# The causal mask of two softmax attentions: a bf16 product on TensorE, or an addition on VectorE

## The chip, the cores and the metric

The kernel runs on one core of a Trainium2 chip. The metric is the device time of one execution in microseconds; the time before is the median of three runs, 904.34 us.

## What is computed

The reference is two hybrid layers in a row on 512 tokens of width 1024. The first mixes a forgetting attention of 8 heads, a pooling branch and a stick-breaking attention of 4 heads; the second mixes an MLA attention of 8 heads with a gated convolution, and then has a feed-forward net. The change touches the two softmax attentions only. Their scores are masked before the softmax:

```python
def forgetting_attention(q, k, v, log_f):
    c = jnp.cumsum(log_f, axis=-1)
    def one_block(args):                      # 128 queries
        qi, ci, i = args
        qpos = i * Q_BLOCK + jnp.arange(Q_BLOCK)
        sc = jnp.einsum('bhqd,bhkd->bhqk', qi, k).astype(jnp.float32) * scale
        sc = sc + (ci[..., :, None] - c[..., None, :])
        sc = jnp.where(kpos[None, :] <= qpos[:, None], sc, NEG)
        p = jax.nn.softmax(sc, axis=-1)
        return jnp.einsum('bhqk,bhkd->bhqd', p.astype(v.dtype), v)

def causal_block_attention(q, k, v):          # the MLA attention, 128 queries a block
    s = jnp.einsum('bqhd,bkhd->bhqk', q_blk, k).astype(jnp.float32) * scale
    s = jnp.where(k_idx[None, :] <= q_idx[:, None], s, jnp.finfo(jnp.float32).min)
    pr = jax.nn.softmax(s, axis=-1)
    return jnp.einsum('bhqk,bkhd->bqhd', pr.astype(v.dtype), v)
```

## The kernel before

Every engine has its own program, written out by hand, and semaphores tie them together. Large products are three fp32r products of split operands (L502, L503, L504: high by high, low by high, high by low). The weights stream from HBM through SyncE's queue; GpSimd splits them into high and low parts (L447, L455) ahead of TensorE.

Each softmax attention is `softmax_attention`, once in the program of TensorE, once in that of ScalarE, once in that of VectorE. It goes over 32 steps `m` (8 heads by 4 blocks of 128 queries); step n counts both attentions together, 0 to 31 for the forgetting attention ("fox") and 32 to 63 for MLA. A step has `kw` = 128, 256, 384 or 512 keys in turn, since a block of queries sees the keys up to its own. The last 128 of them are the diagonal block, the only one that the mask cuts.

In a step TensorE does `scores(m)` (for fox three products L806, L807, L808; for MLA L1079; and then the mask, L726), `turn_probs(m - 3)` (as many 128x128 transposes, L559, as the block has key blocks), and `beside(m)`: three products of another matrix (L502 to L504) that fill the time. After every two heads comes `values` (L747). For the first three steps of an attention there is nothing to transpose. The scores lie in banks 0 to 2 in turn, the transposed probabilities in banks 3 and 4.

VectorE takes the negated maximum of the scores (L2003), and after it, for the step before, the reciprocal of the sum (L2009) and the product with it (L2010, `h`). Besides these it does what is hung between the steps (`fox_pair`, `mix_low`, `sqk_out`, `mla_pair`). ScalarE takes the exponential out of the bank with its sum (L1462, two records) and then copies the transposed probabilities of the step three back out of their bank (L1324, `PT<-bank` or `arena<-bank`). The waits that matter: the maximum waits for `scored` of its step, the exponential for `maxed`, the reciprocal for `exped`, the transposes of a step for `normed` of that step and for `pt_made` of the step two back, the scores for `exped` of the step three back.

The mask is made once by GpSimd (L411, L420): 0 where a key may be seen, -1e30 above the diagonal, in bf16. `ident_b` is the identity in bf16, so the product L726 adds the mask to the bank.

Of the kernel before, what the change touches and what calls it, by code (L numbers as in the profile page):

```python
# [7 lines left out]
P = 128  # L8
F32 = mybir.dt.float32
F32R = mybir.dt.float32r  # L10
BF16 = mybir.dt.bfloat16
# [11 lines left out]
HD = 64  # L23
# [170 lines left out]
def hybrid_kernel(nc, x_d, w_d, cols_d, pos_d, wpool_d, pt_d, gains_d, out_d):  # L194
    tiles = tile_counts(psum_tiles())
    with ExitStack() as ctx:
# [33 lines left out]
        c_head = sb("c_head", [P, FOX_H], F32R)  # L230
        ident = sb("ident", [P, P])
        ident_b = sb("ident_b", [P, P], BF16)
        mask_le = sb("mask_le", [P, P], BF16)
        mask_lt = sb("mask_lt", [P, P], BF16)
        neg_tri = sb("neg_tri", [P, P])
        neg_one = sb("neg_one", [P, P])
# [94 lines left out]
        sines = sem("sines")  # L331
        angles = sem("angles")

        scored, maxed, exped, normed = sem("scored"), sem("maxed"), sem("exped"), sem("normed")
        turned, pt_made, pv_done, pv_drained = sem("turned"), sem("pt_made"), sem("pv_done"), sem("pv_drained")

        z_full, z_abs, z_exp, z_ln, sp_made = sem("z_full"), sem("z_abs"), sem("z_exp"), sem("z_ln"), sem("sp_made")
# [148 lines left out]
        def _(pe):  # L486
# [226 lines left out]
            def softmax_attention(base, heads, score_, v_, beside, first=None, tail=None):  # L713
                steps = heads * T

                def scores(m):
                    i, qb = m // T, m % T
                    n = base + m
                    if m >= 3:
                        pe.wait_ge(exped, n - 2)  # L720
                    elif first:
                        first(m)
                    out = bank[n % 3]
                    kw = (qb + 1) * P
                    score_(out[:, 0:kw], i, qb, kw)
                    mm(out[:, qb * P:kw], ident_b[:, :], mask_le[:, :], start=False, stop=True).then_inc(scored, 1)  # L726

                def turn_probs(m):
                    qb = m % T
# [72 lines left out]
            def fox_score(out, i, qb, kw):  # L802

                at = slice(qb * P, (qb + 1) * P)
                c_at = 0 if qb < 2 else S // 2
                mm(out, q_parts[:, i, at], k_parts[:, i, 0:kw], start=True, stop=False)  # L806
                mm(out, q_swapped[:, i, at], k_parts[:, i, 0:kw], start=False, stop=False)  # L807
                mm(out, c_head[0:HD + FOX_H, i:i + 1].broadcast_to([HD + FOX_H, P]),  # L808
                   c_parts[0:HD + FOX_H, c_at:c_at + kw], start=False, stop=False)

            pe.wait_ge(k_lo, FOX_H)
            pe.wait_ge(q_swapped_in, 32)
# [263 lines left out]
                    out2a_block(0, g, k)  # L1076

            def mla_score(out, i, qb, kw):
                mm(out, q2T[0:QK2, i, qb * P:(qb + 1) * P], k2T[0:QK2, i, 0:kw], start=True, stop=False)  # L1079

            softmax_attention(FOX_H * T, MLA_H, mla_score, v2, out2c_piece,
                              first=lambda m: pe.wait_ge(drained["act"], tiles["q2T", 2][3][1]),
# [711 lines left out]
        def _(dve):  # L1794
# [201 lines left out]
            def softmax_attention(base, heads, pair_out, beside=None, ahead_of_last=None):  # L1996
                steps_ = heads * T
                for m in range(steps_ + 1):
                    if m < steps_:
                        n = base + m  # L2000
                        kw = (m % T + 1) * P
                        dve.wait_ge(scored, n + 1)
                        V.tensor_reduce(negmax[:, n % 8:n % 8 + 1], bank[n % 3][:, 0:kw], AX_X, ALU.max, negate=True)\  # L2003
                            .then_inc(maxed, 1)
                    if m > 0:
                        n = base + m - 1
                        kw = ((m - 1) % T + 1) * P
                        dve.wait_ge(exped, n + 1)
                        own(V.reciprocal(erec[:, n % 8:n % 8 + 1], esum[:, n % 8:n % 8 + 1]))  # L2009
                        V.tensor_scalar(P_buf[:, n % 4, 0:kw], P_buf[:, n % 4, 0:kw], erec[:, n % 8:n % 8 + 1],  # L2010
                                        None, ALU.mult).then_inc(normed, 1)

                    if m % (2 * T) == T + 1 and m > 2 * T:
                        pair_out(m // (2 * T) - 1)
                    if beside is not None:
                        beside(m)
                if ahead_of_last is not None:
                    ahead_of_last()
                pair_out(heads // 2 - 1)
# [463 lines left out]
```

## Time and profile before

| | us |
|---|---|
| median of 3 runs | 904.34 (904.05 to 904.45) |
| the profiled execution, its own time | 904.17 |
| its span, first to last instruction | 902.4 |
| TensorE busy in it | 895.1 (99%) |
| VectorE, ScalarE, GpSimd busy | 390.9, 342.4, 496.0 |
| granted clock of TensorE | 1.00 |
| fox attention, first to last mask | 147.5 to 201.7 |
| MLA attention, first to last mask | 391.3 to 447.2 |

The first number of a row of the timeline is the start in us from the span's start, the second the record's length. A record of TensorE is longer than what it keeps the engine: products overlap, and what a product costs is read from the start of one to the start of the next.

### The profile page before, as it was taken

To read this page: it belongs to the slowest core of one execution; us is meant where nothing else is said; L and a number is where in the kernel's file an instruction comes from. 1 tells how busy PE (TensorE), PEld (TensorE's weight loads), DVE (VectorE), ACT (ScalarE), POOL (GpSimd) and SP (SyncE) were. 2 spreads that over 40 slices of the span, in tenths; PEclk is the share of its full clock that TensorE was granted. 3 is DMA by queue.
4 is the path that set the end of the run, shared out by engine and by line. 5 is a ranking of instruction groups with operands and counts; after the bars stand their busy time and mean duration, and the time that the engine had idled before them with its cause. 6 is when DMAs were issued, how large, how long until landed. Compare 5 with 4: busy or idle time off the path is not lost. (4 is left out here: it accounts for less than half of the span.)

```text
span 902.4 us, 12927 instructions
## 1 busy us (share of the span) xinstructions
PE 895.1 (99%) x4528; PEld 737.3 (82%) x4528; DVE 390.9 (43%) x684; ACT 342.4 (38%) x693; POOL 496.0 (55%) x515
## 2 busy tenths in 40 slices
PE   8999999999999999999999999999999999999998
PEld 7889887777779888876679988888888888888887
DVE  2753494667743652755657611111111122223672
ACT  4333403556726221565648522222222223223421
POOL 7987794311565877923236454444444455555453
PEclk9999999999999999999999999999999999999999
DMA  6335522103122322321012332222232322222213
GB/s 218 120 137 130 141 104 94 47 25 117 72 70 71 117 98 90 110 77 47 12 48 97 107 136 93 93 93 93 100 105 97 117 94 93 93 96 105 74 53 117
DMA packets 28412, 85.73 MB, mean 95 GB/s; under 512 B 5064, under 2 KB 8016, under 8 KB 28240
## 3 DMA queue, kind: packets, MB, share of 16 engines
q1 hardware_dynamic: 24528, 78.65, 25.3%
q10 hardware_dynamic: 3840, 6.48, 2.5%
q8 instruction: 29, 0.48, 0.2%
q14 instruction: 15, 0.12, 0.1%
HBM read 80.93 MB, written 2.10 MB: 92 GB/s over the span
## 5 line engine op out<-in xcount | busy, mean ns | idle before, releaser
L455 POOL TENSOR_TENSOR w_lo<-raw,w_hi 128x256 fp32r<-128x256 f32 (+1 forms) x420 | 409.2, 1002 | 206.5 <-ACT w_hi L1324 200.6
L502 PE MATMUL bank<-aT_hi,w_hi 128*128 128x512 f32 (+1 forms) x584 | 225.7, 387 | 0.0
L504 PE MATMUL bank<-aT_hi,w_lo 128*128 128x512 f32 (+1 forms) x584 | 222.4, 381 | 0.0
L503 PE MATMUL bank<-aT_lo,w_hi 128*128 128x512 f32 (+1 forms) x584 | 222.2, 381 | 0.0
L502 PE MATMUL bank<-w_hi,aT_hi 128*128 128x512 f32 (+3 forms) x576 | 218.5, 379 | 0.7 <-POOL w_lo L455 0.7
L504 PE MATMUL bank<-w_hi,aT_lo 128*128 128x512 f32 (+3 forms) x576 | 213.2, 370 | 0.0
L503 PE MATMUL bank<-w_lo,aT_hi 128*128 128x512 f32 (+3 forms) x576 | 212.9, 370 | 0.0
L447 POOL TENSOR_SCALAR w_hi<-raw 128x1024 fp32r<-128x1024 f32 x70 | 76.3, 1091 | 180.2 <-PE bank L504 143.9
L1324 ACT ACTIVATE w_hi<-raw 128x1024 fp32r<-128x1024 f32 x70 | 74.2, 1060 | 232.2 <-PE bank L504 220.0
L504 PEld LDWEIGHTS bank<-aT_hi,w_lo 128*128 128x128 f32 x584 | 109.8, 188 | 21.0
L503 PEld LDWEIGHTS bank<-aT_lo,w_hi 128*128 128x128 f32 x584 | 110.0, 188 | 19.9 <-issue 0.2
L502 PEld LDWEIGHTS bank<-aT_hi,w_hi 128*128 128x128 f32 x584 | 110.0, 188 | 19.7 <-issue 0.2
L502 PEld LDWEIGHTS bank<-w_hi,aT_hi 128*128 128x128 f32 x576 | 108.5, 188 | 19.3 <-issue 1.6
L504 PEld LDWEIGHTS bank<-w_hi,aT_lo 128*128 128x128 f32 x576 | 108.3, 188 | 18.4
L503 PEld LDWEIGHTS bank<-w_lo,aT_hi 128*128 128x128 f32 x576 | 108.6, 189 | 16.0
L2339 DVE TENSOR_TENSOR aT_lo<-arena,aT_hi 128x512 fp32r<-128x512 f32 x22 | 27.3, 1250 | 78.0 <-ACT aT_hi L1324 78.0
L2328 DVE TENSOR_TENSOR arena<-arena,bank 128x512 f32 (+1 forms) x22 | 15.1, 688 | 93.4 <-PE bank L504 90.6
L2325 DVE TENSOR_TENSOR arena<-bank,R 128x512 f32<-128x512 f32 x22 | 15.2, 692 | 88.3 <-PE bank L504 87.8
L1462 ACT ACTIVATE h<-bank,negmax 128x128 f32<-128x128 f32 (+1 forms) x64 | 33.9, 529 | 44.4 <-DVE negmax L2003 43.9
L2003 DVE TENSOR_REDUCE negmax<-bank 128x1 f32<-128x128 f32 (+1 forms) x64 | 31.1, 488 | 34.9 <-PE bank L726 33.8
L1324 ACT ACTIVATE arena<-bank,stat 128x512 f32<-128x512 f32 (+3 forms) x32 | 19.6, 612 | 45.4 <-PE bank L504 42.3
L1810 DVE SCALAR_TENSOR_TENSOR aT_lo<-bank,g_col,aT_hi 128x256 fp32r<-128x256 f32 (+3 forms) x41 | 20.4, 527 | 23.8 <-ACT aT_hi L1324 22.0
(235 smaller groups left out, 921.6 us busy)
## 6 DMA issues: line engine op xcount, KB each, us to landing
raw<-in_weights SPq DMA_DIRECT2D x141, 512.0 KB, 3.2
q_swapped<-q_parts ACTq DMA_DIRECT2D x2, 1024.0 KB, 12.5
x<-in_x ACTq DMA_DIRECT2D x4, 512.0 KB, 5.2
y_out<-x SPq DMA_DIRECT2D x7, 256.0 KB, 4.0
x<-in_x SPq DMA_DIRECT2D x3, 512.0 KB, 7.8
g_post<-in_gains ACTq DMA_DIRECT2D x3, 512.0 KB, 3.4
x<-in_x SPq DMA_DIRECT2D x2, 256.0 KB, 3.7
raw<-in_weights SPq DMA_DIRECT2D x2, 256.0 KB, 4.7
```

What stands on the lines that cost most here:

```text
L447: nc.gpsimd.tensor_scalar(w_hi[:, s, :], raw[:, r, :], 1.0, 1.0, ALU.mult, ALU.mult).then_inc(hi_made, 1)
L455: lo = nc.gpsimd.tensor_tensor(w_lo[:, s, at], raw[:, r, at], w_hi[:, s, at].bitcast(F32), ALU.subtract)
L502: mm(out, st_hi, mv_hi, start=start, stop=False)
L503: mm(out, st_hi, mv_lo, start=False, stop=False)
L504: return mm(out, st_lo, mv_hi, start=False, stop=stop)
L1324: return A(out, in_, ACT.Copy, scale=scale)
L1462: A(P_buf[:, n % 4, 0:kw], bank[n % 3][:, 0:kw], ACT.Exp, bias=negmax[:, n % 8:n % 8 + 1], accum_out=esum[:, n % 8:n % 8 + 1]).then_inc(ex ...
L1810: return V.scalar_tensor_tensor(out=out, in0=in0, scalar=scalar, in1=in1, op0=op0, op1=op1)
L2003: V.tensor_reduce(negmax[:, n % 8:n % 8 + 1], bank[n % 3][:, 0:kw], AX_X, ALU.max, negate=True)\
L2325: V.tensor_tensor(sg_t[:, slot, :], bank[2 * slot][:, :], R[:, :], ALU.mult).then_inc(ffn_scaled, 1)
L2328: V.tensor_tensor(act[:, bass.ds(f, 1), :], sg_t[:, slot, :].unsqueeze(1), bank[2 * slot + 1][:, :].unsqueeze(1), ALU.mult).then_inc(ffn_a ...
L2339: V.tensor_tensor(aT_lo[:, slot, :].unsqueeze(1), act[:, bass.ds(k, 1), :], aT_hi[:, slot, :].bitcast(F32).unsqueeze(1), ALU.subtract).the ...
```

## The change

The product L726 goes, and with it the last weight load of each score. The last product of the scores itself closes the group and signals `scored`: `fox_score` and `mla_score` now return it. `mask_le` becomes fp32. In VectorE's program each step now begins with an addition of the mask, in place, onto the last 128 columns of the bank, and the maximum waits for it by a new semaphore, `masked`. The same product of the stick-breaking attention (`mask_lt`, L829) stays.

```diff
-        mask_le = sb("mask_le", [P, P], BF16)
+        mask_le = sb("mask_le", [P, P])
...
-                    score_(out[:, 0:kw], i, qb, kw)
-                    mm(out[:, qb * P:kw], ident_b[:, :], mask_le[:, :], start=False, stop=True).then_inc(scored, 1)
+                    score_(out[:, 0:kw], i, qb, kw).then_inc(scored, 1)
...
-                mm(out, c_head[0:HD + FOX_H, i:i + 1].broadcast_to([HD + FOX_H, P]),
-                   c_parts[0:HD + FOX_H, c_at:c_at + kw], start=False, stop=False)
+                return mm(out, c_head[0:HD + FOX_H, i:i + 1].broadcast_to([HD + FOX_H, P]),
+                          c_parts[0:HD + FOX_H, c_at:c_at + kw], start=False, stop=True)
...
-                mm(out, q2T[0:QK2, i, qb * P:(qb + 1) * P], k2T[0:QK2, i, 0:kw], start=True, stop=False)
+                return mm(out, q2T[0:QK2, i, qb * P:(qb + 1) * P], k2T[0:QK2, i, 0:kw], start=True, stop=True)
...
                         dve.wait_ge(scored, n + 1)
+                        own_keys = bank[n % 3][:, kw - P:kw]
+                        V.tensor_tensor(own_keys, own_keys, mask_le[:, :], ALU.add).then_inc(masked, 1)
+                        dve.wait_ge(masked, n + 1)
                         V.tensor_reduce(negmax[:, n % 8:n % 8 + 1], bank[n % 3][:, 0:kw], AX_X, ALU.max, negate=True)\
                             .then_inc(maxed, 1)
```

In the changed kernel line numbers are higher by one from L334 on and by three behind the addition: L2003 becomes L2006, and the addition is L2004.

TensorE, fox steps 3 and 4, before:

```order
L808 MATMUL bank0<-c_parts,c_head 128x512
L726 MATMUL bank0<-mask_le,ident_b 128x128
L559 MATMUL bank3<-ident,h 128x128
L502 MATMUL bank7<-aT_hi,w_hi 128x512
L503 MATMUL bank7<-aT_lo,w_hi 128x512
L504 MATMUL bank7<-aT_hi,w_lo 128x512
L806 MATMUL bank1<-k_parts_51,q_parts_50 128x128
L807 MATMUL bank1<-k_parts_51,q_swapped_52 128x128
L808 MATMUL bank1<-c_parts,c_head 128x128
L726 MATMUL bank1<-mask_le,ident_b 128x128
L559 MATMUL bank4<-ident,h 128x128 x2
```

and in the changed kernel:

```order
L808 MATMUL bank0<-c_parts,c_head 128x512
L560 MATMUL bank3<-ident,h 128x128
L503 MATMUL bank7<-aT_hi,w_hi 128x512
L504 MATMUL bank7<-aT_lo,w_hi 128x512
L505 MATMUL bank7<-aT_hi,w_lo 128x512
L806 MATMUL bank1<-k_parts_51,q_parts_50 128x128
L807 MATMUL bank1<-k_parts_51,q_swapped_52 128x128
L808 MATMUL bank1<-c_parts,c_head 128x128
L560 MATMUL bank4<-ident,h 128x128 x2
```

The transposes now stand right behind the last product of the scores; nothing else moved.

VectorE, the end of fox (steps 28 to 31), before:

```order
L2003 TENSOR_REDUCE negmax<-bank2 128x1
L2009 RECIPROCAL erec<-esum 128x1
L2010 TENSOR_SCALAR h<-h,erec 128x128
L2026 TENSOR_TENSOR arena<-bank6,arena 128x512
L1842 TENSOR_TENSOR aT_lo<-arena,aT_hi 128x512
L2003 TENSOR_REDUCE negmax<-bank0 128x1
L2009 RECIPROCAL erec<-esum 128x1
L2010 TENSOR_SCALAR h<-h,erec 128x256
L2003 TENSOR_REDUCE negmax<-bank1 128x1
```

and in the changed kernel:

```order
L2004 TENSOR_TENSOR bank2<-bank2,mask_le 128x128
L2006 TENSOR_REDUCE negmax<-bank2 128x1
L2012 RECIPROCAL erec<-esum 128x1
L2013 TENSOR_SCALAR h<-h,erec 128x128
L2029 TENSOR_TENSOR arena<-bank6,arena 128x512
L1842 TENSOR_TENSOR aT_lo<-arena,aT_hi 128x512
L2004 TENSOR_TENSOR bank0<-bank0,mask_le 128x128
L2006 TENSOR_REDUCE negmax<-bank0 128x1
L2012 RECIPROCAL erec<-esum 128x1
L2013 TENSOR_SCALAR h<-h,erec 128x256
L2004 TENSOR_TENSOR bank1<-bank1,mask_le 128x128
L2006 TENSOR_REDUCE negmax<-bank1 128x1
```

Each maximum has an addition in front of it; the order is otherwise the same.

## Rows read from the trace of the kernel before

**Rows 1.** The page, busy time, share of the span and instructions of each engine.

```profile
PE 895.1 (99%) x4528; PEld 737.3 (82%) x4528; DVE 390.9 (43%) x684; ACT 342.4 (38%) x693; POOL 496.0 (55%) x515
```

**Rows 2.** Timeline of TensorE in fox: start, length, line, out<-in; mask products of two steps.

```profile
152.64 0.27 PE L807 MATMUL bank<-k_parts,q_swapped 128*128 128x128 f32 x1
152.75 0.27 PE L808 MATMUL bank<-c_parts,c_head 72*128 72x128 f32 x1
...
157.80 0.23 PE L726 MATMUL bank<-mask_le,ident_b 128*128 128x128 bf16 x1
157.87 0.28 PE L559 MATMUL bank<-ident,h 128*128 128x128 f32 x1
...
158.22 0.40 PE L503 MATMUL bank<-aT_lo,w_hi 128*128 128x512 f32 x1
```

**Rows 3.** Timeline of TensorE, transposes without a mask product ahead.

```profile
16.07 1.04 PE L559 MATMUL bank<-ident,x 128*128 128x128 f32 x8
...
17.17 0.39 PE L503 MATMUL bank<-w_lo,aT_hi 128*128 128x512 f32 x1
```

**Rows 4.** Timeline of TensorE in MLA, a step with one transpose.

```profile
401.94 0.22 PE L726 MATMUL bank<-mask_le,ident_b 128*128 128x128 bf16 x1
...
402.34 0.39 PE L503 MATMUL bank<-w_lo,aT_hi 128*128 128x512 f32 x1
```

**Rows 5.** Timeline of TensorE, bf16 mask products back to back.

```profile
208.80 0.62 PE L829 MATMUL bank<-mask_lt,ident_b 128*128 128x128 bf16 x8
```

**Rows 6.** Groups of VectorE by form: count, busy us, mean ns, idle us before them.

```profile
L2339 DVE TENSOR_TENSOR aT_lo<-arena,aT_hi 128x512 fp32r<-128x512 f32 x22 | 27.3, 1250 | 78.0 <-ACT aT_hi L1324 78.0
L2328 DVE TENSOR_TENSOR arena<-arena,bank 128x512 f32 x18 | 12.4, 688 | 85.8 <-PE bank L504 85.8
...
L2003 DVE TENSOR_REDUCE negmax<-bank 128x1 f32<-128x128 f32 x16 | 4.6, 289 | 14.7 <-PE bank L726 13.9 <-ACT arena L1443 0.8
...
L2064 DVE TENSOR_TENSOR sp_sum<-PT 128x128 f32<-128x128 f32 x2 | 0.6, 291 | 0.1
```

**Rows 7.** Timeline of VectorE, an instruction that waits for the one before it.

```profile
158.68 0.15 DVE L2009 RECIPROCAL erec<-esum 128x1 f32<-128x1 f32 x1
158.87 0.42 DVE L2010 TENSOR_SCALAR h<-h,erec 128x384 f32<-128x384 f32 x1
```

**Rows 8.** Waits in fox, 147 to 205 us: total us, times, longest.

```profile
DVE negmax L2003 <- PE bank L726: 15.1, 18, 2.5
```

**Rows 9.** Waits in MLA, 391 to 449 us.

```profile
DVE negmax L2003 <- PE bank L726: 18.6, 21, 2.4
```

**Rows 10.** Timeline of ScalarE at the start of fox.

```profile
148.89 1.28 ACT L1479 ACT_TABLE_LOAD   x1
...
153.89 0.27 ACT L1324 ACTIVATE PT<-bank 128x128 f32<-128x128 f32 x1
```

**Rows 11.** Timeline of VectorE at the start of fox.

```profile
150.87 0.78 DVE L2010 TENSOR_SCALAR h<-h,erec 128x128 f32<-128x128 f32 x1
...
152.49 0.68 DVE L2003 TENSOR_REDUCE negmax<-bank 128x1 f32<-128x512 f32 x1
```

**Rows 12.** Timeline of TensorE, the transposes of step 2.

```profile
154.30 0.52 PE L559 MATMUL bank<-ident,h 128*128 128x128 f32 x3
```

**Rows 13.** Timeline of VectorE at the end of fox, maximum of step 30.

```profile
200.41 0.55 DVE L2003 TENSOR_REDUCE negmax<-bank 128x1 f32<-128x384 f32 x1
```

**Rows 14.** Timeline of ScalarE at the end of fox, copy of step 27.

```profile
201.57 0.59 ACT L1324 ACTIVATE PT<-bank 128x512 f32<-128x512 f32 x1
```

**Rows 15.** Timeline of TensorE at the end of fox, transposes of step 29.

```profile
202.59 0.38 PE L559 MATMUL bank<-ident,h 128*128 128x128 f32 x2
```

**Rows 16.** Timeline of VectorE at the start and at the end of MLA.

```profile
392.59 0.16 DVE L1833 TENSOR_TENSOR stat<-stat 128x4 f32<-128x4 f32 x1 [4.59 <-ACT stat L1331]
...
446.64 0.56 DVE L2003 TENSOR_REDUCE negmax<-bank 128x1 f32<-128x384 f32 x1 [0.17 <-DVE arena L2226]
```

**Rows 17.** Timeline of TensorE at the end of MLA, transposes of step 61.

```profile
448.54 0.41 PE L559 MATMUL bank<-ident,h 128*128 128x128 f32 x2 [0.27 <-ACT PT L1324]
```

More of the change, by code:

```diff
@@ L332, in hybrid_kernel @@
         angles = sem("angles")
-        scored, maxed, exped, normed = sem("scored"), sem("maxed"), sem("exped"), sem("normed")
+        scored, masked, maxed = sem("scored"), sem("masked"), sem("maxed")
+        exped, normed = sem("exped"), sem("normed")
         turned, pt_made, pv_done, pv_drained = sem("turned"), sem("pt_made"), sem("pv_done"), sem("pv_drained")
```

## The prediction

> **What bounds the kernel now.** The page comes first: TensorE is busy 99% of the span [rows 1], so the time is TensorE's work plus its few gaps, and every other engine matters only where TensorE comes to wait for it. The timeline of TensorE then shows both attentions without a gap but one, of 0.27 us at the end of MLA [rows 17]. So a step costs what TensorE issues in it. The waits show the other side: the maxima of VectorE wait for the scores for 15.1 us in the 32 steps of fox [rows 8] and for 18.6 us in those of MLA [rows 9], 0.47 and 0.58 us a step. That is the room for what VectorE is given, if it is where it is needed.
>
> **What goes from TensorE.** 64 products of 128 columns with their weight loads. From the start of a mask product to the start of the second product behind it are 0.42 us in fox with one transpose between [rows 2]. Without a mask product ahead, eight transposes and one such product take 1.10 us [rows 3]. With 0.23 us for a 512-column product that is (1.10 - 0.23) / 8 = 0.11 us a transpose and nothing over. So the mask costs 0.42 - 0.11 - 0.23 = 0.08 us, on finer reading 0.074 in every such step of fox; in MLA 0.40 - 0.34 = 0.06, finer 0.064 [rows 4]. [...] At 128 keys in fox less comes free: L807 and L808 start 0.11 us apart [rows 2], twice what 128 columns take [rows 5], so the weight load sets the pace, and the load of the next transpose would show where the mask hid it. I count 0.025 us there. MLA: 32 x 0.064 = 2.05 us, and 0.15 more for its first three steps, where no transposes stand between. Fox, steps 4 to 31: 21 x 0.074 + 7 x 0.025 = 1.7 us. Steps 0 to 3 would give 0.4 us but give nothing: the first exponential waits for a table load that ends at 150.17, and through the reciprocal the product of step 0 ends at 151.65 (150.87 + 0.78), 0.06 us ahead of its transpose, whatever TensorE does [rows 10, 11]. Sum of what TensorE is spared: 3.9 us.
>
> **What VectorE gets.** An addition of 128 columns out of a bank and SBUF into the bank. No row shows VectorE writing a bank. The nearest: an addition of 128 columns in SBUF, 0.291 us, and the maximum over 128 columns of a bank, 0.289 us [rows 6]; so reading a bank costs nothing extra. I take 0.29 us. The maximum then waits for it, and such a wait shows as 0.19 us from start to start behind a record of 0.15 [rows 7], 0.035 us more. So each step's chain gets 0.325 us longer, less 0.07 us since `scored` comes from a product that ends that much sooner. Below, the addition could come to 0.21 us, what a 128-column maximum keeps its successor from starting; above, to 0.45 or more if a write to a bank is dear. On average 0.325 fits under the 0.47 and 0.58 us of idle time. In the steady part nothing is lost then: a step's transposes come three steps after its scores, and the probabilities are ready 1 us or more ahead.
>
> The Trainium skill (Perfetto Trace Analysis, Optimizing Scalar/DVE Operations) gives about 60 ns of access overhead for DVE on SBUF and about 125 ns on PSUM, which speaks against this change. An addition dearer by that 0.065 us would make the time about 903.7; the two rows of 289 and 291 ns do not show it for reads.
>
> **Where it does not fit.** There are four places at which VectorE has no idle time.
> - Start of fox. From 150.87 VectorE runs without a pause [rows 11]. The additions of steps 2 and 3 put the maximum of step 3 from 152.49 to 153.14. Its exponential stands on ScalarE ahead of the copy of step 0, which moves from 153.89 to 154.55 and ends at 154.8 [rows 10], and the transposes of step 2, at 154.30 before, wait for that copy [rows 12]. TensorE is late by 0.5 us there.
> - From step 4 to the end TensorE regains its 0.07 us a step and stands at -1.1 us by step 28. But there VectorE has `mix_low` and `fox_pair` between the steps and no idle time up to the maximum of step 30 [rows 13]. Three additions, 0.98 us, eat what the engine had gained. The exponential of step 30 and the copy of step 27 behind it stay at 201.57 to 202.2 [rows 14], while TensorE would like to turn step 29 at 202.59 - 1.1 = 201.5 [rows 15]. It waits 0.75 us. Fox ends at -0.3 us.
> - Start of MLA. VectorE is held to 392.59 and some more by the chain of the group norm [rows 16] and then works off steps 0 to 3 in a row; four additions less its 0.6 us of pauses make TensorE wait 0.2 us.
> - End of MLA. TensorE waits there already [rows 17], for the copy of step 59 behind the exponential of step 62, which waits for a maximum that stands behind `mla_pair` [rows 16]. Two more additions, less 0.14 us for the sooner scores, put it 0.5 us behind TensorE's pace.
> MLA ends at 2.2 - 0.2 - 0.5 = -1.5 us.
>
> GpSimd makes the mask in fp32 as it makes `neg_tri`, at the same length. Behind the attentions TensorE is the bound again and carries the shift to the end. Sum: -0.3 - 1.5 = -1.8 us. The profiled execution took 904.17 us, 0.17 under the median, so 902.4 on its own scale and **902.5** on that of the runs.
>
> **The rivals.**
> - *The slack covers it all.* If the addition held nobody up, only the table load would cost: 3.9 us gained, 900.4. For it: 15.1 and 18.6 us of waiting. Against it: the four places above, where VectorE has none. A cheap addition (0.21 us) gives part of it, -2.8, 901.6.
> - *Writing the bank is dear.* Followed through the same four places the result moves by 1.0 us from 0.29 to 0.35 us (903.5) and by 1.8 more to 0.45 (905.4, +1.0); break-even is 0.395 us. Nothing in the trace excludes it.
> - *GpSimd doubles the addition: slower.* In the feed-forward net VectorE's subtraction of two SBUF operands takes 1250 ns, the addition with a bank among its operands at the same time 688 [rows 6]. The new addition has a bank, so it should be spared. If it were hit like the first, 0.58 us a piece exceeds the idle time of a step in both attentions, VectorE sets the pace, and fox comes to +3.6, MLA to +1.9: 909.9. It decides from about 0.47 us a piece on, where the result passes +1.8.
> - *Only the stream comes free.* If the gaps around the mask product stay (0.055 us a step regained), the sum is 0.0 for fox and -1.2 for MLA, 903.1.
>
> **How the numbers follow.** My forecast has 0.52, and its own range is 901.7 to 903.2; the cheap or covered addition has 0.15 (900.4 to 901.7); the dear one 0.18 (903.2 to 905.4); the doubled one 0.10 (906 to 910); the stream alone 0.05. A measurement of this kernel tells 0.2% from no change, 1.8 us: 902.53 and 906.15 are the bounds, and my forecast stands on the first. Half of its chance is faster: 0.26 + 0.15, and a little of the rest, 0.43. Slower: 0.10. The same: 0.47. The range reaches from 900.8 to 905.2 and leaves out the doubled addition and the full gain.
>
> **What would show it.** In the changed profile: the addition at 0.29 us and the maximum 0.325 us behind its start; from L808 to the transposes 0.24 us at 512 keys, and 0.34 us from one transpose's start to the second product behind it; the transposes of step 2 near 154.8, those of step 31 near 204.9 (205.21 before); the end of MLA 1.8 us earlier than before; and the attentions' maxima still waiting for L808 and L1079, some 5 us in fox and 9 in MLA. The prediction is wrong if the addition is 0.4 us or more, if TensorE waits for VectorE in the middle of an attention, or if the distance behind L808 doesn't shrink.

## The result

| | before | changed | changed, measured again |
|---|---|---|---|
| median of the runs, us | 904.27 (6) | 909.47 (6) | 907.95 (6), beside 904.57 (20) |
| ratio, 95% interval | | 1.0056 [1.0045, 1.0066] | 1.0037 [1.0024, 1.0050] |
| the profiled execution, us | 904.17 | 910.51 | 907.32 |
| its span, us | 902.4 | 908.8 | 905.6 |

The change makes the kernel slower by 0.4 to 0.6%. One of the six runs in each of the two columns of the changed kernel was disturbed; the ratios leave it out, and without it the medians are 908.80 and 907.35, which is 4.5 and 2.8 us over the kernel before. The prediction, 902.5 with a range up to 905.2, missed it on the wrong side. Most of what the two profiled executions differ by lies in the first ten microseconds, as shown below, so the argument goes mainly by the second, `e1_after_again`. It is the same kernel and is called **the repeat** here.

The page of the changed kernel, busy times, beside [rows 1]:

```profile
PE 895.7 (99%) x4464; PEld 737.1 (81%) x4464; DVE 406.0 (45%) x748; ACT 343.0 (38%) x693; POOL 496.9 (55%) x515
```

64 products are gone from TensorE, and its busy time has not fallen here (in the repeat it is 893.9 us). Of VectorE 64 instructions are new. Its busy time grew by 15.1 us and not by the 18.8 of 64 additions of 0.293 us, because records overlap. The groups of VectorE by form, answering to [rows 6]:

```profile
L2004 DVE TENSOR_TENSOR bank<-bank,mask_le 128x128 f32<-128x128 f32 x64 | 18.8, 293 | 18.3 <-PE bank L1079 9.4 <-PE bank L808 7.0 <-ACT arena L1443 0.8
...
L2013 DVE TENSOR_SCALAR h<-h,erec 128x512 f32<-128x512 f32 x16 | 9.5, 593 | 0.6
L2013 DVE TENSOR_SCALAR h<-h,erec 128x384 f32<-128x384 f32 x16 | 9.3, 578 | 0.6
...
L2006 DVE TENSOR_REDUCE negmax<-bank 128x1 f32<-128x128 f32 x16 | 4.7, 291 | 0.5
```

The addition has the forecast length, 293 ns. What changed unasked is the normalise product `h<-h,erec` of 384 elements: 578 ns in the mean, and 468 in the kernel before. The waits of the changed kernel in fox, 149 to 211 us (before: [rows 8]), and in MLA, 393 to 458 us (before: [rows 9]):

```profile
DVE bank L2004 <- PE bank L808: 7.0, 7, 2.2
...
PEld bank L560 <- DVE h L2013: 4.6, 7, 1.2
...
PE bank L560 <- ACT PT L1324: 1.8, 4, 0.7
```

```profile
DVE bank L2004 <- PE bank L1079: 9.4, 10, 2.0
...
PEld bank L560 <- DVE h L2013: 3.2, 7, 1.1
PE bank L560 <- ACT PT L1324: 1.2, 3, 0.7
```

VectorE's own waiting for scores fell from 15.1 to 7.0 us and from 18.6 to 9.4. TensorE now waits for probabilities and for copies out of the banks in the middle of both attentions. Before, no transpose in fox waited for either; in MLA weight loads waited 1.7 us for probabilities, which cost TensorE's products nothing, and one product waited 0.3 us for a copy.

**Where the time went.** The same TensorE instruction can be found in two traces (mask products left out) and its start compared. These are the starts against the kernel before, in us, at seven places of the program; the columns are differences, so what a stretch costs is one column less the one before it.

| kernel | fox starts (147) | fox ends (209) | MLA starts (391) | MLA ends (455) | 885 | 890 | end |
|---|---|---|---|---|---|---|---|
| changed | +2.14 | +5.07 | +5.08 | +4.65 | +5.01 | +6.43 | +6.43 |
| the repeat | -0.25 | +2.78 | +2.79 | +2.27 | +2.19 | +3.23 | +3.24 |

Four pieces: the first ten microseconds (+2.1 or -0.3), fox (+2.9 and +3.0), MLA (-0.4 and -0.5), and five microseconds in the last weights of the kernel (+1.4 and +1.0). Between these the shift moves by 0.4 us at most.

### The profile page after: what moved, and what is told of

It is laid out like the page before. It is cut to its first block and busy times, and to the rows that moved or that the text cites. A ratio compares the mean times of both kernels' runs of the same rounds, so it can differ in the third digit from the quotient of the medians.

```text
span 908.8 us, 12863 instructions
## 1 busy us (share of the span) xinstructions
PE 895.7 (99%) x4464; PEld 737.1 (81%) x4464; DVE 406.0 (45%) x748; ACT 343.0 (38%) x693; POOL 496.9 (55%) x515
## 5 line engine op out<-in xcount | busy, mean ns | idle before, releaser
L505 PEld LDWEIGHTS bank<-w_hi,aT_lo 128*128 128x128 f32 x576 | 108.3, 188 | 18.6
L2342 DVE TENSOR_TENSOR aT_lo<-arena,aT_hi 128x512 fp32r<-128x512 f32 x22 | 27.3, 1250 | 78.0 <-ACT aT_hi L1324 78.0
L2331 DVE TENSOR_TENSOR arena<-arena,bank 128x512 f32 (+1 forms) x22 | 15.1, 688 | 92.6 <-PE bank L505 90.0
L2006 DVE TENSOR_REDUCE negmax<-bank 128x1 f32<-128x128 f32 (+1 forms) x64 | 31.4, 491 | 2.2
```

The costliest lines, as they stand in the source:

```text
L505: return mm(out, st_lo, mv_hi, start=False, stop=stop)
L2331: V.tensor_tensor(act[:, bass.ds(f, 1), :], sg_t[:, slot, :].unsqueeze(1), bank[2 * slot + 1][:, :].unsqueeze(1), ALU.mult).then_inc(ffn_a ...
L2342: V.tensor_tensor(aT_lo[:, slot, :].unsqueeze(1), act[:, bass.ds(k, 1), :], aT_hi[:, slot, :].bitcast(F32).unsqueeze(1), ALU.subtract).the ...
```

## The first ten microseconds belong to the execution

TensorE's first products of 512 columns, in the kernel before and in the changed one:

```profile
6.42 1.19 PE L614 MATMUL bank<-w_hi,aT_hi 128*128 128x512 f32 x4 [0.73 <-POOL w_hi L432]
```

```profile
7.03 2.08 PE L615 MATMUL bank<-w_hi,aT_hi 128*128 128x512 f32 x4 [0.73 <-POOL w_hi L433]
```

Four of them take 1.19 us in one and 2.08 in the other, 0.23 and 0.43 us apart: 512 columns in 0.43 us is the level of 1.2 GHz, in 0.23 us that of 2.4. In both traces TensorE had done small transposes since 1.60. In the kernel before they went from 0.21 to 0.11 us apart at 4.98; in the changed one they stayed at 0.21, and the pace rose only past 10 us. A profile's table by stretches gives a granted clock of 1.00 for both, but the clock records in the traces tell them apart: the first record, at 1.00, starts at 4.92 us in the kernel before and at 10.20 in the changed one, where the pace rises, and ahead of it there is none. In the repeat it starts at 5.92, and the repeat had the fast pace. In the padded kernel below it starts at 10.08, and that kernel has the same start as the changed one (+1.96). Not all of the 2.1 us is the clock: 0.6 of it was there when the first of these products started (7.03 instead of 6.42), because GpSimd's split waited for a load of weights until 6.36 instead of 5.74.

Single executions of the kernel before stand about 1.5 us above its median too (905.87 and 906.01 beside 904.57). So 2.1 of the 6.4 us of the profiled execution are no effect of the change. What decides when the clock rises wasn't tried.

## Is it the attentions, and which engine?

Four kernels on one chip. The repeat has no edit.

> The changed kernel once more, unchanged. In its first profile TensorE is later than before by 2.07 us at 10 us (before the attentions), by 4.8 behind the fox attention, by 4.8 behind MLA, and by 6.4 at the end. Theory A (the loss belongs to the attentions, the rest comes and goes from run to run): the shift over fox and MLA is again 2.7 us, +-0.2, and the 2.07 us at the start and the 1.3 us at the last weights are there in some executions and not in others, so that the times spread from about 907 to 910.5. Theory B (all of it belongs to the changed program): all 6.4 us come again, in the same places.

The masks in both types, new semaphore and buffers in place, but the mask a bf16 product as before:

```
-    score_(out[:, 0:kw], i, qb, kw).then_inc(scored, 1)
+    last = score_(out[:, 0:kw], i, qb, kw, False)
+    last = mm(out[:, qb * P:kw], ident_b[:, :], mask_le_b[:, :], start=False, stop=True)
+    last.then_inc(scored, 1)
...
-    V.tensor_tensor(own_keys, own_keys, mask_le[:, :], ALU.add).then_inc(masked, 1)
-    dve.wait_ge(masked, n + 1)
```

> The mask stays a product on TensorE in all 64 steps; from the change only the fp32 mask (beside a bf16 one), the new semaphore and the shifted buffers are there. Theory A: 904.3, no shift anywhere. Theory B': the buffers' places or GpSimd's two more mask instructions (0.5 us at 22 us) make the lost 2 us at the start or the 1.3 us at the end: 906 to 907.5.

Neither product nor addition (the edit above without its `+` product), so it leaves out the mask:

> No mask at all in the two softmax attentions: neither the product nor the addition, so their results are those of an unmasked softmax. It measures what TensorE is spared. By the prediction's sum 3.9 us come free and both attentions stay without waits for VectorE: 900.4. If only the stream of the product comes free: 901.1. If something else than the addition costs the time: not under 904.

Both, product and addition:

> Mask product on TensorE and addition on VectorE, both in every step (the mask is added twice, which changes nothing after the softmax). VectorE's queue as in the changed kernel, TensorE's pace as before. If TensorE simply waits for a VectorE that is full, the attentions take what they take in the changed kernel, +2.7 us or less than 1 us more: 907 to 908. If the waits are a latency on top of TensorE's own work, the product's 4 us come back in full: 911.

| kernel | median, us | ratio, 95% interval | fox | MLA | 885 to 890 |
|---|---|---|---|---|---|
| e1, the repeat | 907.95 | 1.0037 [1.0024, 1.0050] | +3.03 | -0.52 | +1.04 |
| e2, product, new layout | 904.46 | 0.9998 [0.9988, 1.0007] | 0.00 | -0.01 | 0.00 |
| e3, neither | 902.03 | 0.9971 [0.9960, 0.9981] | -1.89 | -2.00 | +1.69 |
| e4, both | 909.18 | 1.0049 [1.0035, 1.0064] | +3.81 | +0.74 | +0.14 |

The kernel before was at 904.57 beside them. The layout costs nothing. Taking the product away spares TensorE 3.89 us in the two attentions, which is the 3.9 of the prediction's sum; that e3 takes 902.03 and not the 900.4 expected of it is the 1.69 us in the last weights. The addition then costs 4.92 us in fox and 1.48 in MLA. With the product put back beside it (e4) only 2.04 of the 3.89 us come back, 0.78 in fox and 1.26 in MLA, between the two cases of its expectation: part of the product's time falls into TensorE's waits. Theory A is right for the attentions and the start, wrong for the last weights: they lose in e1 and e3, not in e2 and e4, so the loss goes with the absence of the 64 products from TensorE's stream.

## What costs 5 us in fox

The trace answers by the eight-step period in which GpSimd splits one chunk of weights. From one maximum over 512 keys to that of eight steps later (steps 7, 15, 23) it is 14.64 us before, 14.06 without a mask, 15.10 in the repeat. Against the kernel without a mask, TensorE in the repeat is late by 0.66 us at the start of fox, by 1.0 to 1.2 more in each of three periods, by 0.9 at its end. The kernel before, GpSimd's split at its first meeting with VectorE (the 384-wide product that it meets is in [rows 7], from 158.87), and the 512-wide product behind that:

```profile
159.05 1.16 POOL L447 TENSOR_SCALAR w_hi<-raw 128x1024 fp32r<-128x1024 f32 x1 [7.48 <-PE bank L504]
```

```profile
159.81 0.68 DVE L2010 TENSOR_SCALAR h<-h,erec 128x512 f32<-128x512 f32 x1
```

The repeat, the same split and VectorE beside it:

```profile
159.29 1.06 POOL L448 TENSOR_SCALAR w_hi<-raw 128x1024 fp32r<-128x1024 f32 x1 [7.96 <-PE bank L505]
160.43 3.00 POOL L456 TENSOR_TENSOR w_lo<-raw,w_hi 128x256 fp32r<-128x256 f32 x4
```

```profile
159.46 1.10 DVE L2013 TENSOR_SCALAR h<-h,erec 128x384 f32<-128x384 f32 x1
...
161.19 0.95 DVE L2013 TENSOR_SCALAR h<-h,erec 128x512 f32<-128x512 f32 x1
```

Before, the 384-wide product started 0.18 us ahead of `w_hi` and took 0.42 us; `w_hi` took 1.16 instead of 1.06. Now the addition has put it 0.35 us later against the split, it starts 0.17 us behind `w_hi`, and it ends 0.21 us behind `w_hi`'s end (160.35): it waited for the whole instruction. The product over 512 takes 0.49 us where it meets nothing. Before, it met the end of `w_hi` and took 0.68; now it meets the parts of `w_lo` and takes 0.95. The Trainium skill (SBUF — State Buffer, "SBUF: two separate sides") states a rule: a VectorE operation in a mode that uses both its ports and a GpSimd operation exclude each other for a whole instruction, and whichever starts first has the ports. The trace agrees: 1.10 us behind, 0.42 ahead. That this product is in such a mode is concluded from these times; no row names the mode.

What it does to TensorE in the next period, in the repeat:

```profile
178.94 0.39 PE L808 MATMUL bank<-c_parts,c_head 72*128 72x512 f32 x1
179.64 0.30 PE L560 MATMUL bank<-ident,h 128*128 128x128 f32 x1 [0.31 <-ACT PT L1324]
180.24 0.40 PE L505 MATMUL bank<-aT_hi,w_lo 128*128 128x512 f32 x1
180.95 0.64 PE L747 MATMUL bank<-arena 128*64 128x512 f32 x1 [0.32 <-ACT PT L1324]
```

The transpose starts 0.70 us behind L808; where nothing waits it is 0.24. It waits for the copy out of its bank, which stands on ScalarE behind an exponential:

```profile
178.55 0.47 ACT L1462 ACTIVATE h<-bank,negmax 128x256 f32<-128x256 f32 x1 [1.58 <-DVE negmax L2006]
```

The exponential waited for its maximum, which stood on VectorE behind the two long products (1.10 and 0.95 us) and the operation of `fox_pair`. Such pairs of waits stand at 164, 179 and 194 us.

Four kernels test that. Beside e5 to e8 the kernel before took 904.29 us, beside e9 to e12 904.21, beside e13 and e14 904.19. In the first, GpSimd waits for the 384-wide product:

```
+    if out1_at <= c < out1_at + 4:
+        pool.wait_ge(normed, 8 * (c - out1_at) + 7)
     split(c, c % SLOTS, False, parts=4)
```

> The changed kernel, with one more wait: in fox's attention GpSimd starts the split of a weight chunk (w_hi, then four parts of w_lo) only once the 384-wide normalise product of that moment is done (steps 7, 15, 23, 31). In the kernel before this product started 0.18 us ahead of w_hi and took 0.42 us; with the addition it starts 0.17 us behind it and takes 1.10. Theory C (the phase): VectorE's product meets the split because the addition put it 0.35 us later, and waits for w_hi's end; that is what costs fox its time. With the split behind it the product takes 0.42 again, TensorE's eight-step period falls from 15.1 us to 14.1-14.5 (before: 14.6), and fox's stretch costs +0.3 to +1.3 against the kernel before instead of +2.9 and +3.0: 904.5 to 906.5 us. Rival D (the load): VectorE has eight additions of 0.325 us in each period and too little idle time whatever the phase is: the period stays at 15.0-15.1, fox at +2.7 to +3.0, 907.5 to 908.2 us.

906.92 us, ratio 1.0031 [1.0020, 1.0042]; fox +1.91, period 14.79. The edit did what it says, the 384-wide product takes 0.42, but the next one meets `w_hi` in its place:

```profile
159.45 0.42 DVE L2038 TENSOR_SCALAR h<-h,erec 128x384 f32<-128x384 f32 x1
160.51 0.91 DVE L2038 TENSOR_SCALAR h<-h,erec 128x512 f32<-128x512 f32 x1
```

```profile
160.09 1.05 POOL L460 TENSOR_SCALAR w_hi<-raw 128x1024 fp32r<-128x1024 f32 x1 [8.76 <-DVE h L2038]
```

The direction is theory C's, the amount between the two. The next kernel cuts the split up, so that its pieces start behind VectorE's products:

```
     pool.wait_ge(normed, at + 8)                # ahead of w_hi
...
+    if step is not None and n in (0, 2):        # n: part of w_lo
+        pool.wait_ge(normed, min(step + (9 if n == 0 else 10), 4 * T * 2))
```

> The changed kernel with GpSimd's split of fox's four chunks cut up: w_hi only behind the 512-wide normalise product of step 7 (15, 23, 31), two parts of w_lo behind the next one (128-wide), two behind the one after it (256-wide), so that fewer of VectorE's products meet it. Theory C (the meeting is what costs): from fox's +3.0 us (as it was) and +1.9 (split 0.6 us later, where the 512-wide product still took 0.91 and the 128-wide one 0.70 us) to +0.0 to +1.0, the 384- and 512-wide products at 0.42 and about 0.55 us, period 14.2 to 14.5; 905.2 to 906.2 us. Rival D' (what remains of +1.9 is the load of the additions and the two ends): fox stays at +1.6 to +2.0, the period at 14.7 to 14.8 as with the later split, 906.6 to 907.1 us.

```profile
159.35 0.42 DVE L2042 TENSOR_SCALAR h<-h,erec 128x384 f32<-128x384 f32 x1
...
160.41 0.49 DVE L2042 TENSOR_SCALAR h<-h,erec 128x512 f32<-128x512 f32 x1
```

```profile
161.11 1.05 POOL L460 TENSOR_SCALAR w_hi<-raw 128x1024 fp32r<-128x1024 f32 x1 [9.88 <-DVE h L2042]
```

```profile
163.45 0.83 DVE L2042 TENSOR_SCALAR h<-h,erec 128x256 f32<-128x256 f32 x1
```

Fox comes to -0.29 us and the period to 14.04, that of the kernel without a mask (14.06): all eight additions of a period are then free. Rival D', the load of the additions, falls. What is left against the kernel without a mask, 1.6 us, is 0.6 at the start of fox and 1.0 at its end. The meetings are not all gone, though: the parts of `w_lo` now meet the next 256- and 384-wide products, which take 0.83 and 0.68 us instead of 0.35 and 0.42, and there it costs nothing. The time, 905.03 us (ratio 1.0009 [0.9999, 1.0018]), is 0.2 us under theory C's range, although the last weights took +2.08; that piece follows below.

Is the meeting the cause by itself? A kernel with the mask on TensorE, in which GpSimd waits (`pool.wait_ge(exped, 8 * (c - out1_at) + 8)`) until it falls on a product:

> No addition at all: the mask is TensorE's product, as in the kernel before, but in fox's attention GpSimd's split of a chunk waits until ScalarE has summed step 7's (15, 23, 31) exponentials, so that w_hi starts just ahead of VectorE's 512-wide normalise product instead of 0.6 us earlier. That product then waits for w_hi's end: 1.3-1.5 us instead of 0.68. It asks what the meeting costs without the addition. Theory C1 (VectorE's idle time of 0.4 to 0.9 us in a step takes one delay): fox's stretch costs 0.0 to +0.5 us in all, time 904.3 to 904.9. Rival C2 (TensorE waits for that very product whatever idle time follows): +0.5 to +0.7 for each of four, fox +2.0 to +2.8, 906.3 to 907.2 us.

```profile
158.49 0.42 DVE L2038 TENSOR_SCALAR h<-h,erec 128x384 f32<-128x384 f32 x1
159.43 1.32 DVE L2038 TENSOR_SCALAR h<-h,erec 128x512 f32<-128x512 f32 x1
```

```profile
159.42 1.05 POOL L460 TENSOR_SCALAR w_hi<-raw 128x1024 fp32r<-128x1024 f32 x1 [8.20 <-ACT h L1483]
```

903.92 us, ratio 0.9996 [0.9987, 1.0006]; fox -0.03, period 14.65. The product takes 1.32 us, the longest of all these kernels, and costs nothing. C1 is right, its range for the time 0.4 us too high. So a meeting without additions (e9) costs the steady part of fox nothing, and neither do the additions with the shorter meetings moved (e10). What costs is the additions together with the long meeting at the place where the change put it; VectorE's idle time does not cover both there.

The last of the four shortens the addition, and so leaves out most of the mask:

```
-    own_keys = bank[n % 3][:, kw - P:kw]
-    V.tensor_tensor(own_keys, own_keys, mask_le[:, :], ALU.add).then_inc(masked, 1)
+    own_keys = bank[n % 3][:, kw - 8:kw]
+    V.tensor_tensor(own_keys, own_keys, mask_le[:, P - 8:P], ALU.add).then_inc(masked, 1)
```

> The changed kernel, but each addition takes 8 columns of the diagonal block instead of 128 (the other 120 stay without a mask, so the output is not the reference's; the softmax then spans keys it should not see). What a shorter instruction is worth: the add of 128 columns takes 0.28-0.30 us; with 8, if 120 elements cost 0.125 us, 0.16 to 0.18, and with the wait 0.20 us a step instead of 0.325. Theory C (a threshold): the 384-wide product then starts 0.18 us ahead less 0.20, near a tie with w_hi; if ahead, 0.42 us and fox at -0.5 to +0.8; if behind, 1.1 us and fox +1.8 to +2.5. Rival D (the load): fox falls smoothly with the length, from +3.0 to about +1.1 (between -1.9 without and +3.0 with the addition at 0.325). The last weights keep their +1.0 to +1.4 us (no padding). Time 904.5 to 907 us.

```profile
173.85 1.05 POOL L460 TENSOR_SCALAR w_hi<-raw 128x1024 fp32r<-128x1024 f32 x1 [10.68 <-PE bank L517]
173.89 1.22 DVE L2032 TENSOR_SCALAR h<-h,erec 128x384 f32<-128x384 f32 x1
```

906.13 us, ratio 1.0019 [1.0010, 1.0029]; fox +1.73, MLA -1.47, period 14.84. The addition takes 0.15 to 0.17 us. The product misses by 0.04 us: it starts just behind `w_hi` and takes 1.22. With half the addition fox costs 3.6 us over the kernel without a mask (4.9 with the whole): theory C had +1.8 to +2.5 for a product that starts behind, rival D +1.1. It is nearer to C and just under its range, so a part does fall with the length, and in MLA, where fewer splits fall, the shorter addition costs 0.5 instead of 1.5 us.

By attention: the addition in fox alone (`n < 32`) or in 24 steps of MLA alone, with TensorE's product elsewhere.

> The addition on VectorE in fox's 32 steps alone, MLA's mask stays a bf16 product on TensorE. If the two attentions' costs are independent: fox +2.9 us as in the changed kernel, MLA 0.0 (+-0.1) instead of -0.45. The rest depends on the fetch: 64 instructions fewer put it about 6 us behind its old place, to about 878 and 903 us: by theory E between 0 and +1.2 us in the last weights. Sum: 904.6 + 2.9 + 0 to 1.2 = 907.5 to 908.7 us. Rival: fox's loss is partly a drift that the MLA attention takes back whatever its own mask does; then MLA shows -0.3 to -0.5 here too, and the time is under 907.5.

> A version meant to beat both: the addition on VectorE only in MLA's steps 36 to 59 (its third last quarter and the middle), where VectorE showed idle time, everything else a product on TensorE, and two padding increments where a product went, so that the fetches stay in place. Theory (from the landmarks of the changed kernel: MLA -0.45 us with about +0.4 at its start and +0.3 at its end, TensorE's product worth 0.064 us a step): fox 0.0, MLA -24 x 0.064 = -1.5 at best, -1.0 if one wait remains, last weights +0.0 to +0.2; 903.0 to 903.8 us. Rival: the padding or the meeting with GpSimd's splits at 415-423 and 445-453 takes half of it: 904.0 to 904.6 us, no difference that can be measured.

Fox only: 907.40 us, ratio 1.0035 [1.0022, 1.0047]; fox +3.01, MLA 0.00, last weights -0.04. The two attentions are independent; no drift is given back. MLA's middle: 903.63, ratio 0.9988 [0.9979, 0.9998]; fox -0.01, MLA -0.95. It gains 0.7 us, 0.1%, under what a measurement of this kernel tells from nothing with ease. The time of fox alone is 0.1 us under its range, since its last weights cost nothing.

## What costs 1 to 2 us in the last weights

The last weight chunks come to GpSimd as they land, and TensorE waits for them. In every kernel whose TensorE stream is shorter by the 64 products and their 64 weight loads it waits longer there. The trace shows TensorE's instructions arriving by transfers of 16 KB (queue q8), about 25 us apart in this part. In the kernel before they fall at 869.8 and 894.8 us; in the repeat at 860.2 and 884.1, in the middle of the last load of `raw`, and that one takes 2.08 us where the others behind 700 us take 0.9 to 1.4. The trace does not name the engine of q8; that its transfers move by half their distance when 128 instructions of TensorE go tells it. The test is to make the stream as long as before:

```
     last.then_inc(scored, 1)
+    for _ in range(2):
+        pe.sem_inc(pads, 1)
```

> The changed kernel with 128 more instructions in TensorE's stream, two increments of an unused semaphore where each mask product and its weight load stood, so that the stream is as long as before. Theory E (the fetch): without these 128 instructions a 16 KB fetch of instructions falls at 884 to 887 us into the last weight loads (2.1-2.2 us long where others take 0.9-1.4) and TensorE waits for w_lo; with them the fetches fall at about 873 and 898, the stretch 885 to 890 loses 0.0 to 0.3 us instead of 1.0 to 1.7, and the time is 906.2 to 907.3 us, if an increment costs TensorE nothing. Rival F (the state of the queues): the loss comes with the mask's place on VectorE or with when the attentions end, not with the stream's length: +1.0 or more again, 907.6 to 908.6 us. The increments themselves: if each delays TensorE by 0.02 us or more, the attentions lose 2.5 us or more beyond +2.3.

906.91 us, ratio 1.0031 [1.0021, 1.0042]. The time lies in theory E's range, but alone it does not tell this kernel from the repeat (1.0037 [1.0024, 1.0050], on another chip). The trace does: its fetches fall at 874.4 and 899.3 us, the stretch 885 to 890 takes +0.13 instead of +1.04, and the attentions take +2.97 and -0.50 as in the repeat, so an increment costs TensorE nothing that shows. That is what theory E forecast. Two more kernels, since the padding might cure something else. The kernel before with the same 128 increments added, and e10 padded:

> The kernel before, mask on TensorE, with 128 increments of an unused semaphore added to TensorE's stream, two behind each step's mask product. Theory E (the fetch): a fetch brings 256 instructions and they lie 25 us apart there; 128 more put them as far from their old places (869.8 and 894.8 us) as 128 fewer did, so one falls at 882 to 883 us, takes 1.9 to 2.3 us and costs 1.0 to 2.1 us in the stretch 885 to 890, with nothing changed in either attention: 905.2 to 906.6 us. Rival F: the loss needs the changed kernel (the missing products, or an earlier end of the attentions); then 885 to 890 loses under 0.3 us and the time is 904.2 to 904.8 us.

> The changed kernel with all 64 additions, with both cures: GpSimd's splits cut up behind VectorE's products in fox, and TensorE's stream padded back to its old length. Theory C with E: fox -0.3 us and MLA -0.4 as in the run with the split cut up, last weights 0.0 to +0.2 instead of the +2.1 of that run: 903.3 to 903.9 us, the change just a gain. Rival G: the last weights' +2.1 of that run came from the cut-up splits and not from the fetch at 881.7; then it stays above +1.0 and the time is 904.6 to 905.3.

GpSimd's last split, TensorE's wait for it, the fetch and the load (these two of the window 878 to 892 us): in e10, then in e14, then in e13.

```profile
886.06 1.05 POOL L460 TENSOR_SCALAR w_hi<-raw 128x1024 fp32r<-128x1024 f32 x1 [2.70 <-DMA raw<-in_weights]
...
889.75 0.50 PE L525 MATMUL bank<-w_hi,aT_hi 128*128 128x512 f32 x1 [1.83 <-POOL w_lo L471]
...
q8 instruction: 1, 0.02, 0.9%
raw<-in_weights SPq DMA_DIRECT2D x1, 512.0 KB, 6.0
```

```profile
883.93 1.05 POOL L462 TENSOR_SCALAR w_hi<-raw 128x1024 fp32r<-128x1024 f32 x1 [0.69 <-DMA raw<-in_weights]
...
raw<-in_weights SPq DMA_DIRECT2D x1, 512.0 KB, 3.9
```

```profile
885.46 1.05 POOL L448 TENSOR_SCALAR w_hi<-raw 128x1024 fp32r<-128x1024 f32 x1 [1.03 <-DMA raw<-in_weights]
...
889.18 0.50 PE L503 MATMUL bank<-w_hi,aT_hi 128*128 128x512 f32 x1 [0.21 <-POOL w_lo L456]
...
q8 instruction: 1, 0.02, 0.5%
raw<-in_weights SPq DMA_DIRECT2D x1, 512.0 KB, 4.3
```

In a row of a transfer the last number is the microseconds from issue to landing. With the fetch in it the load takes 6.0 us and TensorE waits 1.83; with the stream padded and the splits the same, 3.9 us and no wait: e14 loses +0.10 there, and rival G falls. 903.65 us, ratio 0.9993 [0.9983, 1.0002]: 0.5 us under the kernel before beside it, where e10 was 0.8 over its own.

e13 is 905.01 us, ratio 1.0006 [0.9997, 1.0016]. Up to 885 us it stands at -0.04, nothing in either attention has changed; its fetch falls at 882.0 as expected, and 885 to 890 takes +0.44. So the loss needs no changed mask, and rival F's "under 0.3" is passed; but this fetch took 1.15 us, not 2, the loss is half of the least that theory E gave, and the time lies between the two ranges. Counted from the shift of the program, the fetches that hurt fell 881.9 to 882.8 us into it (six kernels: +1.0 to +2.1); that of e7, 64 instructions shorter, at 879.1 with 0.93 us and no loss. Its fetch came 1.9 us ahead of the issue of the last load, those that hurt 0.9 to 1.8 us behind it.

How much is lost is the extra time of that one load, in every kernel:

| kernel | last load, issue to landing, us | 885 to 890 |
|---|---|---|
| the nine kernels without a fetch in it | 3.79 to 3.99 | -0.04 to +0.14 |
| e13 | 4.29 | +0.44 |
| e5 | 4.89 | +1.03 |
| e1, the repeat | 4.92 | +1.04 |
| e12 | 5.09 | +1.22 |
| changed | 5.31 | +1.42 |
| e3 | 5.57 | +1.69 |
| e10 | 5.95 | +2.08 |

The kernel before has 3.86. The place is settled; why the fetch itself takes 1.15 us in one kernel and 2 in the others, and the load between 4.3 and 6.0, stays open.

## A version faster than both

The addition only where VectorE has room (`4 <= n < 28 or 36 <= n < 60`), the split cut up, the stream padded:

> All that was found, in one version: the addition in steps 4 to 27 and 36 to 59 alone (the first and last four steps of each attention keep the product on TensorE), the split cut up as in the run beside this one, two padding increments where a product went. By theory C and E: fox -1.3 to 0.0 us (24 x 0.074 = 1.8 at best, less what waits remain), MLA -0.95 as measured, last weights 0.0 to +0.2: 902.2 to 903.5 us against 904.3 to 904.6 before. Rival D': fox keeps +0.6 to +1.2 (what remained with the split later, +1.9, less the ends), 904.0 to 904.8 us, no gain over the kernel before and slower than the one with MLA's middle alone (903.63).

901.86 us beside 904.21, ratio 0.9972 [0.9960, 0.9983]; fox -1.53, MLA -0.96, last weights +0.03; the best of all kernels here that compute the whole, and 0.3 us under the range that theories C and E gave. So the addition on VectorE can be worth 2.3 us, with three things done beside it. The cut-up split with the whole mask on TensorE was not run; in the kernel before no product of TensorE waits in fox, so there is nothing seen there that it could give.

## Why the prediction was wrong

- **What TensorE is spared, 3.9 us.** Right: 3.89 (e3), 1.89 in fox (1.7 forecast) and 2.00 in MLA (2.2).
- **The addition, 0.29 and 0.325 us.** Right: 0.293 us, and the maximum starts 0.32 to 0.34 behind it. The starts and lengths in the repeat, at the place of [rows 11]:

```profile
151.33 0.29 DVE L2004 TENSOR_TENSOR bank<-bank,mask_le 128x128 f32<-128x128 f32 x1
151.65 0.56 DVE L2006 TENSOR_REDUCE negmax<-bank 128x1 f32<-128x384 f32 x1
```

  The rivals "writing the bank is dear" and "GpSimd doubles the addition" are out: it has 0.28 to 0.30 us everywhere, also beside `w_lo`. The sum worked out for the second, 909.9, is nearest to the first measurement, and that is luck: it had +3.6 and +1.9 us in the attentions, where +3.0 and -0.5 were measured, and 2.1 us of that execution are its first ten microseconds. What was right in it is that GpSimd holds up VectorE, but another operation than the addition.
- **"In the steady part nothing is lost."** This step failed, and it carries the miss in fox: 3 periods of 1.0 to 1.2 us, +3.0 us for the attention instead of -0.3. It compared an average of idle time (0.47) with an average of work (0.325), and took for granted that VectorE's other operations keep their length when they move. The comparison itself comes out once the splits are moved (e10, period 14.04); what does not hold is the length, 1.10 us instead of 0.42 for the 384-wide product and 0.95 instead of 0.68 for the 512-wide. The product L2010 reads and writes SBUF as the subtraction of 1250 ns in [rows 6] does, which the prediction had quoted, and applied to the addition alone. The row of GpSimd's split, 0.18 us behind that product, was in the trace and not looked for.
- **Start of fox, 0.5.** 0.66. The transposes of step 2, at 154.30 in [rows 12], wait for the copy as forecast (in the repeat, which starts 0.25 us sooner):

```profile
154.73 0.52 PE L560 MATMUL bank<-ident,h 128*128 128x128 f32 x3 [0.51 <-ACT PT L1324]
```

- **End of fox, 0.75.** The wait is there at that size, answering to [rows 15]; against the kernel without a mask the end costs 0.9.

```profile
205.32 0.41 PE L560 MATMUL bank<-ident,h 128*128 128x128 f32 x2 [0.75 <-ACT PT L1324]
```

- **MLA, -1.5 us.** -0.5. The product gave 2.0 of the 2.2 us; the start cost 0.50 (0.2 forecast), the end 0.36 (0.5), and two places that were not in the sum 0.42 and 0.13. With the addition in steps 36 to 59 alone (e8) these two stay: -0.95 instead of -1.5. The larger is this, in the repeat: two operations hung between the steps leave the maximum no room, as at the end of MLA, one head pair earlier.

```profile
431.74 0.75 DVE L1810 SCALAR_TENSOR_TENSOR aT_lo<-bank,cols,aT_hi 128x512 fp32r<-128x512 f32 x1
432.41 0.68 DVE L2229 TENSOR_TENSOR arena<-arena 128x512 f32<-128x512 f32 x1
433.27 0.30 DVE L2004 TENSOR_TENSOR bank<-bank,mask_le 128x128 f32<-128x128 f32 x1 [0.17 <-DVE arena L2229]
```

```profile
435.50 0.41 PE L560 MATMUL bank<-ident,h 128*128 128x128 f32 x2 [0.22 <-ACT PT L1324]
```

- **"Carries the shift to the end."** Wrong by 1.0 to 1.4 us, by a resource that no term of the sum had: the length of the instruction stream.
- **The whole.** The misses are 3.3 us in fox, 1.0 in MLA and 1.0 in the last weights. With the forecast of -1.8 that is +3.5, what the repeat's trace shows behind its first ten microseconds (+3.24 against -0.25).
- **The distances** behind L808 (0.24 us at 512 keys) are right where nothing waits:

```profile
203.36 0.40 PE L808 MATMUL bank<-c_parts,c_head 72*128 72x512 f32 x1
203.60 0.27 PE L560 MATMUL bank<-ident,h 128*128 128x128 f32 x1
```

The prediction named its own falsifier, that TensorE waits for VectorE in the middle of an attention, and it is what happened.

## What to carry to other kernels

When work is added to an engine, don't set its average against the engine's average idle time: go through one period and look at which operations of other engines start within the added delay, above all GpSimd's beside VectorE products that have no operand in a bank. Whoever starts first wins a whole instruction, so a shift of 0.35 us made one product 0.7 us longer here, and ordering waits on GpSimd, which had idle time, took it back for nothing. A change in the number of instructions moves every later fetch; where a kernel waits for its last loads, see what the fetches fall on.

## What the runs showed of the hardware

- The order of two starts decides: the 384-wide product takes 0.42 us when it starts 0.18 us ahead of GpSimd's 1.05 us instruction (before), 1.10 when 0.17 us behind it (e1), 1.22 when 0.04 us behind (e12).
- Adding two increments of a semaphore to each of 64 steps of TensorE costs no time that shows in the attentions (e6, e13), but moves a 16 KB fetch by 12 us.
- Behind 700 us a fetch of 16 KB that falls into the last load takes 1.15 to 2.3 us against 0.9 to 1.4, and that load of 512 KB 4.3 to 6.0 us from issue to landing against 3.8 to 4.0.
- TensorE's first products run at either of two paces, 0.23 or 0.43 us for 512 columns, in different executions. The first clock record of the trace starts where the pace rises, at 4.92 us in the kernel before and at 10.20 in the changed one; with weights that land 0.6 us later this makes 2.1 us.
